# Hybrid decoder step with experts, one core: the last rows' matmuls in another order, the sample rows' norm on GpSimd, their stores on two queues

## What is computed

```python
gates = einsum('btk,btke->bte', top_p, one_hot(top_i, 8))     # two experts per token
for e in range(8):
    y = y + gates[..., e:e + 1] * swiglu(x, w1[e], w3[e], w2[e])
x = layer_norm(ALPHA * x + y, ln_ffn_g, ln_ffn_b)             # (x - mean) * rsqrt(var + eps) * g + b
```

## Time and profile before

| | us |
|---|---|
| median of 3 runs | 1082.62 |
| lowest, highest | 1078.73, 1083.17 |
| the profiled execution, its own time | 1083.95 |
| its span, from the first instruction to the last | 1082.1 |
| TensorE busy in the span | 1058.8 (98%) |
| VectorE, ScalarE, GpSimd busy | 323.9, 170.5, 76.5 |

### The profile page before, as it was taken

The page is one execution under the profiler, slowest core; times in us unless marked ns, Lnnn a source line. Parts: engine busy times, 40 slices in busy tenths (PEclk is TensorE's granted clock), DMA queues, the critical chain, the costliest instruction groups (busy, mean ns, idle before and its releaser), DMA issues.

```text
span 1082.1 us, 21010 instructions
## 1 busy us (share of the span) xinstructions
PE 1058.8 (98%) x9679; PEld 752.9 (70%) x9679; DVE 323.9 (30%) x687; ACT 170.5 (16%) x360; POOL 76.5 (7%) x94
## 2 busy tenths in 40 slices
PE   8999999999999999999999999999999999999995
PEld 6787766987777777897876767844556566566552
DVE  4755635330000000137546443442011010110125
ACT  1322233030000000024222222220000000000011
POOL 1010122000000000000010310041000020000020
PEclk9999999999999999999998999999999999999998
DMA  8452239122344602403421345779999999999972
GB/s 318 149 195 79 78 106 349 70 79 104 130 155 155 263 30 107 190 1 117 184 90 45 120 137 235 291 291 362 398 404 425 398 399 402 425 422 397 406 272 96
DMA packets 36541, 240.08 MB, mean 222 GB/s; under 512 B 4768, under 2 KB 8096, under 8 KB 16736
## 3 DMA queue, kind: packets, MB, share of 16 engines
q1 hardware_dynamic: 26896, 216.40, 51.2%
q0 software_dynamic: 6416, 19.52, 5.1%
q10 hardware_dynamic: 3136, 2.75, 0.8%
HBM read 228.60 MB, written 13.07 MB: 223 GB/s over the span
## 4 chain that ended last, share of the span: by engine, by line
PE 93%; DVE 4%; ACT 1%; issue 1%; DMA 1%; DVEq 0%; SPq 0%; ACTq 0%
PE ps L593 92%; PE ps L596 1%; DMA up_slots<-in_w_in 1%; ACT overlay L1369 1%; DVE overlay L1710 0%; ACT L1369 0%; DVE tables L2230 0%; DVE tables L2312 0%; ACT up_slots L1369 0%; DVE overlay L1969 0%; DVE overlay L1839 0%; DVE up_slots L1810 0%; DVE overlay L1935 0%; DVE mix_or_moe L1837 0%; DVE overlay L1838 0%
## 5 line engine op out<-in xcount | busy, mean ns | idle before, releaser
L593 PE MATMUL ps<-x,up_slots 128*128 128x288 f32 (+2 forms) x1712 | 408.0, 395 | 2.6 <-DMA up_slots<-in_w_in 1.7
L593 PEld LDWEIGHTS ps<-x,up_slots 128*128 128x128 f32 x1712 | 308.4, 191 | 88.0 <-issue 10.3
L593 PE MATMUL ps<-up_slots,mix_or_moe 128*32 128x352 f32 (+2 forms) x3248 | 246.4, 451 | 1.9 <-issue 1.6
L593 PEld LDWEIGHTS ps<-up_slots,mix_or_moe 128*32 128x32 f32 (+2 forms) x3248 | 123.7, 111 | 115.6 <-issue 29.2
L593 PE MATMUL ps<-overlay,up_slots 128*128 128x288 f32 (+2 forms) x824 | 150.2, 344 | 1.0 <-ACT overlay L1369 1.0
L593 PEld LDWEIGHTS ps<-overlay,up_slots 128*128 128x128 f32 x824 | 128.3, 191 | 22.6 <-ACT overlay L1369 1.9
L593 PE MATMUL ps<-overlay,tables 128*32 128x256 f32 (+4 forms) x2012 | 125.7, 375 | 0.5 <-DVE overlay L1704 0.5
L593 PEld LDWEIGHTS ps<-overlay,tables 128*32 128x32 f32 (+2 forms) x2012 | 87.2, 114 | 36.3 <-issue 3.6
L1369 ACT ACTIVATE overlay<-ps 128x288 f32<-128x288 f32 (+3 forms) x77 | 33.5, 435 | 389.5 <-PE ps L593 389.5
L2269 DVE TENSOR_TENSOR mix_or_moe<-mix_or_moe,ps 128x352 f32<-128x352 f32 x24 | 11.2, 517 | 182.0 <-PE ps L593 182.0
L521 POOL TENSOR_TENSOR up_slots<-mix_or_moe,tables 32x2048 f32<-32x2048 f32 x6 | 21.7, 3620 | 543.4 <-ACT mix_or_moe L1369 543.4
(11 more groups left out here) (282 smaller groups left out, 621.7 us busy)
## 6 DMA issues: line engine op xcount, KB each, us to landing
up_slots<-in_moe_w SPq DMA_DIRECT2D x64, 1408.0 KB, 16.6
overlay<-in_moe_w SPq DMA_DIRECT2D x21, 1536.0 KB, 16.9
up_slots<-in_ffn_w SPq DMA_DIRECT2D x30, 1024.0 KB, 7.0
up_slots<-in_w_in SPq DMA_DIRECT2D x27, 1024.0 KB, 5.0
up_slots<-in_w_out SPq DMA_DIRECT2D x8, 1024.0 KB, 9.1
overlay<-in_moe_w SPq DMA_DIRECT2D x7, 1024.0 KB, 18.8
mix_or_moe<-in_states POOLq DMA_DIRECT2D x6, 512.0 KB, 10.9
out_sample_states<-mix_or_moe POOLq DMA_DIRECT2D x6, 512.0 KB, 6.1
```

The costliest lines, as they stand in the source:

```text
L593: return pe.matmul(o, lhsT, rhs, start=start, stop=stop)
```

## The change

Four things change, all behind expert 7's second projection.

1. `last_rows` is cut in three. `first_rows(g)` is tokens 0 to 127, `later_rows(g, cs)` tokens 128 to 255 for the listed quarters, `sample_rows(g)` the sample tokens. The order becomes: down 0 and 1, `first_rows(0)`, five of the eleven steps of down 2, `first_rows(1)`, the other six steps, then for `g` 0 and 1 the quarters 0, 1 and 3 of the later tokens and the sample tokens, `first_rows(2)` (`comb_ps` 1), quarter 2 of groups 0 and 1 (bank 2 holds the down product of group 2 until ScalarE has copied it), all quarters of group 2, and the sample tokens of group 2 (`comb_ps` 2).
2. The sample tokens are summed in the upper half of bank 3, not 4.
3. VectorE's last norm keeps only the prompt tokens: first pass and reciprocal of tile 0, first pass and reciprocal of tile 1, second pass of tile 0, the reciprocal of the sample tokens, second pass of tile 1. The passes over `ZLAST` go to GpSimd as four instructions (add the negative mean, times `g`, times the reciprocal, plus `b`), each of which waits for the one before. The third waits for VectorE's third reciprocal (`z_rs` 3).
4. `y_rows` becomes three semaphores. SyncE stores two quarters of `y_sample`, ScalarE the other two.

```diff
...
@@ -492,11 +492,11 @@
                 sp.dma_start(ZLAST[GT * c:GT * c + GT, :], XTK[0:NS, 2, CO * c:CO * c + CO]).then_inc(S["sample_in"], 16)
             yp = out["y_prompt"].rearrange("a (t p) d -> (a t) p d", p=P)
             for t in range(2):
-                sp.wait_ge(S["y_rows"], t + 1)
+                sp.wait_ge(S[f"y_rows_{t}"], 1)
                 sp.dma_start(yp[t], XTK[:, t]).then_inc(S["y_stored"], 16)
-            sp.wait_ge(S["y_rows"], 3)
+            sp.wait_ge(S["y_rows_2"], 1)
             ys = out["y_sample"].rearrange("b t d -> (b t) d")
-            for c in range(NCH):
+            for c in range(2):
                 sp.dma_start(ys[:, CO * c:CO * c + CO], ZLAST[GT * c:GT * c + GT, :]).then_inc(S["y_stored"], 16)
             sp.wait_ge(S["y_stored"], 16 * (2 + NCH))
 
@@ -584,6 +584,17 @@
             for t in (2, 0, 1):
                 rows_back(0, t, S[f"glo_in_{t}"])
                 rows_back(1, t, S[f"ghi_in_{t}"])
+            pool.wait_ge(S["ln_rows_in"], 32 * (1 + NCH))
+            pool.wait_ge(S["z_xc"], 3)
+            pool.wait_ge(S["z_total"], 2)
+            pool.tensor_scalar(ZLAST, ZLAST, ZMEAN[:, 2:3], None, ALU.add).then_inc(S["z_step"], 1)
+            pool.wait_ge(S["z_step"], 1)
+            pool.tensor_tensor(ZLAST, ZLAST, LNLAST[:, 0], ALU.mult).then_inc(S["z_step"], 1)
+            pool.wait_ge(S["z_step"], 2)
+            pool.wait_ge(S["z_rs"], 3)
+            pool.tensor_scalar(ZLAST, ZLAST, ZSD[:, 2:3], None, ALU.mult).then_inc(S["z_step"], 1)
+            pool.wait_ge(S["z_step"], 3)
+            pool.tensor_tensor(ZLAST, ZLAST, LNLAST[:, 1], ALU.add).then_inc(S["y_rows_2"], 1)
             pool.wait_ge(S["states_stored"], 16 * DEPTH * STORES)
 
 
@@ -1239,29 +1250,36 @@
                                       W3[k][:, CH * j:CH * j + CH], k == 0, k == KT - 1)
                     last.then_inc(S["u3_last"], 1)
 
-            def last_rows(g):
+            groups = [slice(GT * c, GT * c + GT) for c in range(NCH)]
+
+            def first_rows(g):
                 if g == 0:
                     pe.wait_ge(S["gt_ready"], 1)
                     pe.wait_ge(S["moe_h"], NG * NE)
                 pe.wait_ge(S["y_last"], g + 1)
-                groups = [slice(GT * c, GT * c + GT) for c in range(NCH)]
                 for c, r in enumerate(groups):
-                    mm(PS[:, 4 + c, 0:CO], GTR[g][r, 0:P], YLAST[r, g], g == 0, g == NG - 1 and c > 0)
-                for c, r in enumerate(groups):
-                    last = mm(PS[r, 4, CO:2 * CO], GTR[g][r, SEQ:T], YLAST[r, g], False, g == NG - 1)
+                    last = mm(PS[:, 4 + c, 0:CO], GTR[g][r, 0:P], YLAST[r, g], g == 0, g == NG - 1)
                 if g == NG - 1:
                     last.then_inc(S["comb_ps"], 1)
-                    for i in range(NG):
-                        for c, r in enumerate(groups):
-                            last = mm(PS[:, c, 0:CO], GTR[i][r, P:SEQ], YLAST[r, i], i == 0, i == NG - 1)
-                    last.then_inc(S["comb_ps"], 1)
+
+            def later_rows(g, cs):
+                for c in cs:
+                    last = mm(PS[:, c, 0:CO], GTR[g][groups[c], P:SEQ], YLAST[groups[c], g], g == 0, g == NG - 1 and c < 3)
+                return last
+
+            def sample_rows(g):
+                for r in groups:
+                    last = mm(PS[r, 3, CO:2 * CO], GTR[g][r, SEQ:T], YLAST[r, g], False, g == NG - 1)
+                return last
 
             def last_down():
                 for g in range(NG):
                     if g == 2:
-                        last_rows(0)
+                        first_rows(0)
                     pe.wait_ge(S["ht_done"], NG * (NE - 1) + g + 1)
                     for i in range(FT):
+                        if i == 5 and g == 2:
+                            first_rows(1)
                         if i % 3 == 0 and g == 0:
                             pe.wait_ge(*w2_part(NE - 1, i // 3))
                         for c in range(NCH):
@@ -1303,8 +1321,14 @@
                         down(e - 1, a)
                 pe.wait_ge(S["y_ev"], NG * (NE - 1))
                 last_down()
-                last_rows(1)
-                last_rows(2)
+                for g in range(2):
+                    later_rows(g, (0, 1, 3))
+                    sample_rows(g)
+                first_rows(2)
+                for g in range(2):
+                    later_rows(g, (2,))
+                later_rows(2, range(NCH))
+                sample_rows(2).then_inc(S["comb_ps"], 1)
                 sample_sums()
             with pe.Else():
                 pe.wait_ge(S["gate_row"], 1)
@@ -1571,6 +1595,10 @@
                 f(GHI[:, 2, 0:CO], ZLAST, ACT.Square, bias=ZMEAN[:, 2:3], accum_out=ZSQ[:, 2:3]).then_inc(S["z_total"], 1)
                 act.wait_ge(S["zs_ps"], 2)
                 f(ZSD[:, 2:3], PS[:, 7, CO + 1:CO + 2], ACT.Sqrt, bias=LN_EPS).then_inc(S["z_sd"], 1)
+                act.wait_ge(S["y_rows_2"], 1)
+                ys = out["y_sample"].rearrange("b t d -> (b t) d")
+                for c in range(2, NCH):
+                    act.dma_start(ys[:, CO * c:CO * c + CO], ZLAST[GT * c:GT * c + GT, :]).then_inc(S["y_stored"], 16)
 
 
             with act.If(sparse):
@@ -2227,19 +2255,18 @@
                 v.wait_ge(S["ln_rows_in"], 32 * (1 + NCH))
                 for t in range(2):
                     v.wait_ge(S["z_sq"], t + 1)
-                    link(stt(XTK[:, t], XTK[:, t], ZMEAN[:, t:t + 1], LNROWS[:, 0], AD, M))
+                    stt(XTK[:, t], XTK[:, t], ZMEAN[:, t:t + 1], LNROWS[:, 0], AD, M).then_inc(S["z_scaled"], 1)
                     if t == 0:
                         v.wait_ge(S["zs_ps"], 1)
                         sig(ts(ZMEAN[:, 2:3], PS[:, 7, CO:CO + 1], -1.0, None, M), S["z_xc"], 3)
-                for t in range(2):
                     v.wait_ge(S["z_sd"], t + 1)
-                    link(v.reciprocal(ZSD[:, t:t + 1], ZSD[:, t:t + 1]))
-                    stt(XTK[:, t], XTK[:, t], ZSD[:, t:t + 1], LNROWS[:, 1], M, AD).then_inc(S["y_rows"], 1)
-                v.wait_ge(S["z_total"], 2)
-                link(stt(ZLAST, ZLAST, ZMEAN[:, 2:3], LNLAST[:, 0], AD, M))
+                    v.reciprocal(ZSD[:, t:t + 1], ZSD[:, t:t + 1]).then_inc(S["z_rs"], 1)
+                v.wait_ge(S["z_rs"], 2)
+                v.wait_ge(S["z_scaled"], 2)
+                stt(XTK[:, 0], XTK[:, 0], ZSD[:, 0:1], LNROWS[:, 1], M, AD).then_inc(S["y_rows_0"], 1)
                 v.wait_ge(S["z_sd"], 3)
-                link(v.reciprocal(ZSD[:, 2:3], ZSD[:, 2:3]))
-                stt(ZLAST, ZLAST, ZSD[:, 2:3], LNLAST[:, 1], M, AD).then_inc(S["y_rows"], 1)
+                v.reciprocal(ZSD[:, 2:3], ZSD[:, 2:3]).then_inc(S["z_rs"], 1)
+                stt(XTK[:, 1], XTK[:, 1], ZSD[:, 1:2], LNROWS[:, 1], M, AD).then_inc(S["y_rows_1"], 1)
 
             before = chain[0]
             with v.If(sparse):
@@ -2312,7 +2339,7 @@
                     link(stt(z, PS[:, bank:bank + 4, 0:CO], 1.0, z, M, AD, accum_out=ZSUM[:, t:t + 1]))
                     sig(ts(ZMEAN[:, t:t + 1], ZSUM[:, t:t + 1], -1.0 / D, None, M), S["z_xc"], t + 1)
                 v.wait_ge(S["sample_in"], 16 * NCH)
-                stt(ZLAST, PS[:, 4, CO:2 * CO], 1.0, ZLAST, M, AD, accum_out=ZSUM[:, 2:3]).then_inc(S["z_total"], 1)
+                stt(ZLAST, PS[:, 3, CO:2 * CO], 1.0, ZLAST, M, AD, accum_out=ZSUM[:, 2:3]).then_inc(S["z_total"], 1)
                 last_norm()
             with v.Else():
                 chain[0] = before
```

More of the change, by code:

```diff
@@ L81 @@
 idx_ready gate_exp x_sent xgt_in_0 xgt_in_1 xe_done d_x d_x_ps u1_step u3_step u3_last ht_done dn_step
-moe_s moe_h y_ev y_last y_sent gh_ready gh_ps gt_ready comb_ps base_ready sample_in z_total zs_ps glo_in_0 glo_in_1 glo_in_2 ln_room dl_step ghi_in_0 ghi_in_1 ghi_in_2 ln_rows_in z_sq z_sd y_rows gate_row d_up
+moe_s moe_h y_ev y_last y_sent gh_ready gh_ps gt_ready comb_ps base_ready sample_in z_total zs_ps glo_in_0 glo_in_1 glo_in_2 ln_room dl_step ghi_in_0 ghi_in_1 ghi_in_2 ln_rows_in z_sq z_sd y_rows_0 y_rows_1 y_rows_2 z_scaled z_rs z_step gate_row d_up
 d_dn d_ye d_gate_ps
```

## The result

| | before | after |
|---|---|---|
| median, us | 1081.24 (21 runs) | 1085.82 (21 runs) |
| lowest to highest | 1078.12 to 1083.36 | 1082.51 to 1087.61 |
| ratio of the medians, 95% interval | | 1.0042 [1.0031, 1.0054] |
| profiled execution: own time, span | 1083.95, 1082.1 | 1082.82, 1081.0 |
| TensorE, VectorE, GpSimd busy in it | 1058.8, 323.9, 76.5 | 1055.4, 323.2, 80.6 |

A forecast was written before the change was run, and what follows sets the result against it. It took TensorE, then VectorE's norm, then the stores as the bound: sums +1.04 us, sample rows at 1079.2 for 1077.33, stores giving back 2.1, span +0.35; on the 1082.62 median that is 1083.0 us, range 1079.5 to 1085.0.

The forecast's parts named there:

- The case "within 0.5%": Whole kernel: the change stays within 5.4 us of no change, either way; chance 0.93.
- part 3: Stores at the end: sample rows ready at 1079.2, last issue 1079.65, landing 1082.05, span end 1082.45.
- the 0.4 us that the end took after the landing before: Close of the span: it ends 0.4 us after the last store lands, as before.
- only three things in this change can move the end: Kernel end: only VectorE's getting its two sums, time until the last norm pass is written, and the stores count.
- Part 1: Matmul order on TensorE: first sum 0.74 us later, second 1.04, whole norm taken as 1.04 later.
- rival D: TensorE: matmuls of other quarters fill the tile-size changes, so the sums come as before and the time is 1082.0; chance 0.13.
- Part 2: Last norm on VectorE and GpSimd: the engines exclude each other, sample rows ready at 1079.2, before at 1077.33.
- rival C: GpSimd norm passes cost more than 0.55 us each and VectorE is held too; at 1.0 us a pass, 1084.8; chance 0.15.
- The lock of the earlier trace: Two-SBUF-input VectorE pass beside a GpSimd add stood still, 3.28 us instead of 0.45; taken to hold both ways.
- Rival B: Last norm: GpSimd and VectorE don't exclude each other, so 1081.7, down to 1080.8; chance 0.22.
- Part 3's other term: Sample stores split over SyncE and ScalarE: last issue 0.4 us after the first instead of 2.52, giving back 2.1 us.

The follow-up runs named there:

- run 1: Changed kernel with the sample passes back on VectorE behind its last prompt pass, matmul order and two-queue stores kept: 1091.09 us, ratio 1.0005 to the kernel before.
- run 3: Kernel before plus one GpSimd multiply pass that nobody waits for, started when VectorE's last pass is done: 1093.92 us, ratio 1.0033.
- 6: Kernel before plus one GpSimd memset that nobody waits for, started when VectorE's last pass is done: 1091.93 us, one execution.
- 7: Kernel before with the fourth sample store issued and waited for by GpSimd instead of SyncE, no late GpSimd computation: 1095.34 us, one execution.
- run 2: Kernel before plus one GpSimd multiply pass that nobody waits for, started early, some 10 us before the end: 1091.49 us, ratio 1.0009.
- run 4: Kernel before with the new matmul order alone, sample sums in bank 3: 1091.75 us, ratio 1.0010.
- run 5: Kernel before with only the sample stores split, two quarters on SyncE and two on ScalarE: 1089.19 us, ratio 1.0001.

## Why the prediction was wrong

Forecast +0.35 us on the profile and 1083.0, measured +4.6 us and 1085.82, above the stated range of 1079.5 to 1085.0. The case "within 0.5%" is the one that came. The 1083.0 stands on a median of three runs, 1082.62, which by chance lay 1.4 us above that of 21; so the 2.8 us by which it missed make the error look smaller than it is, 4.2 us.

**The step that failed** is in part 3: "with the 0.4 us that the end took after the landing before". It was carried over from before to after as if it belonged to the stores. It belonged to whatever engine is last: for SyncE 0.4 us behind the landing, for GpSimd 6.9 behind its last pass. After's 1081.0 - 1076.9 = 4.1 us replaced it, +3.7. Without GpSimd the 0.4 would still not hold, because ScalarE closes at 1077.6: with the 0.3 us from that drain to the end in run 1, I estimate an end near 1077.9 and a tail of 24.6 us. Run 1 measured 24.6. So of the 4.1 us GpSimd's drain makes some 3.1, and the other 1.0 compares with the forecast's 0.35. Already the first paragraph had it wrong, with "only three things in this change can move the end". GpSimd, idle at the end before, became the last engine to compute, and the closing line of before, which the prediction doesn't look at, showed for it a drain of 16 us. Runs 1, 3, 6 and 7 show this cause; run 2 shows that without the lateness it costs nothing in the tail.

**Part 1** was right in kind and a little small. The cut down product with the first rows of group 1 took 5.67 us (1053.90 to 1059.57), forecast 5.70. First sum +0.85 for 0.74, second +1.19 for 1.04; run 4 has the same numbers without the other parts. The weight loader is idle 0.33 to 0.41 us at each change of size, as in the earlier trace rows, so rival D falls.

**Part 2** was right at its end by luck, through two errors against each other. Sample rows 7.41 us after the first norm pass, forecast 7.57. GpSimd was held, which no row of before had shown: the pass of 1068.68 ended 0.8 us after VectorE's of 1067.95 did (1069.22), the pass of 1070.10 ended 0.6 us after VectorE's of 1069.32, and that of 1071.31 0.8 us after VectorE's of 1070.63. Alone, line 597 took 0.72 and the pass of run 3, which is of the other kind, 0.86, so a GpSimd pass is 0.72 to 0.86 and not 0.55 us. That is rival C's direction; its case was worked out at 1.0 us a pass and with VectorE held as well. VectorE, against the forecast, was hardly held: the pass of 1069.32 took 1.31 though GpSimd ran until 1070.02 in it, and the pass of 1070.63 took 1.67; in run 1 the same two took 1.28 and 1.27, so 0.4 us in all. So GpSimd's last pass ended 1.6 us after VectorE's last, where the forecast had about 1. The lock of the earlier trace rows is not the same both ways with passes this short, and run 2 shows the same. Rival B is met on VectorE's side only: GpSimd does wait. The Trainium skill ("SBUF — State Buffer", section "Who interferes with whom") has each block the other for whole instructions; of that the trace bears out GpSimd's side. VectorE's side is borne out by the earlier trace rows but not by the pass of 1069.32.

**Part 3's other term**, the split that "gives back 2.1 us", rested on a cause that wasn't there. In after the time from rows written to landed fell by 1.4 us (4.4 to 3.0), and the forecast's own sum had 1.5 (2.85 after the rows), so in size it came true. But run 5 has the split without the gain (4.2), and run 1 has it without the gain too (4.5). In these two the second issue is held on both queues, in after on neither, and why it isn't held in after stays open. So that agreement is luck. The 1.62 us of one issue in the earlier trace rows, which the forecast left unexplained, fits a hold by the prompt store ahead of it; no run takes that store away, so this isn't shown either. What is shown is that a second issuing engine doesn't remove it. The four sample stores of after landed 1.5 to 2.6 us after their issue, a little sooner than in the earlier trace rows.

## What to carry to other kernels

Before you give late work to an idle engine, look at what that engine does after its last instruction, and compare where the chain of waits stops with the end of the span: here it was 7.1 us after against 4.8 before, and what fills it is stores landing or one engine's closing. In a kernel like this one keep GpSimd's last pass, or its wait for a DMA, at least 7 us ahead of the end, or leave the work where it is. Ahead of the last sums, group matmuls of one tile size instead of alternating sizes, and put behind them what the sums don't need. Price a last store by its landing, which other stores just ahead of it lengthen, and don't expect a second issuing queue to shorten that.
